# Latent projection with four Strassen pairs, and the queries' norm finished one stage later

## What is computed

```python
u = rms_norm(x, p['norm_g']) * (1.0 + scale[:, None]) + shift[:, None]
proj = u @ p['w_in']
q_a, kv_a, k_rope, z_mla, cb, cc, cx, z_conv, rw, z_rw, g_merge = split_cols(proj)
c_q = rms_norm(q_a, p['q_norm_g'])        # 384 columns
...
ckv = rms_norm(kv_a, p['kv_norm_g'])      # 256 columns
kpe = rope(k_rope[:, :, None, :], pos)[:, :, 0]
...
y_mla = (o_mla * jax.nn.silu(z_mla)) @ p['w_mla_out']     # z_mla: 512 columns
```

## Time and profile before

| | |
|---|---|
| median of 3 runs | 3518.74 us (3515.11 to 3522.74) |
| span of the profiled execution | 3519.6 us |
| busy: PE, PEld, DVE, ACT | 3371.0, 2236.2, 1701.1, 960.9 us |
| mean granted clock of TensorE | 0.972 of full speed |

### The profile page before, as it was taken

The page is one execution under the profiler, slowest core; times in us unless marked ns, Lnnn a source line. Parts: engine busy times, 40 slices in busy tenths (PEclk is TensorE's granted clock), DMA queues, the critical chain, the costliest instruction groups (busy, mean ns, idle before and its releaser), DMA issues. The chain is left out here.

```text
span 3519.6 us, 65817 instructions
## 1 busy us (share of the span) xinstructions
PE 3371.0 (96%) x28655; PEld 2236.2 (64%) x28655; DVE 1701.1 (48%) x3191; ACT 960.9 (27%) x2056; POOL 147.7 (4%) x175
## 2 busy tenths in 40 slices
PE   7999999999989999999989999999999999999998
PEld 5677655666556677765656766566665666776665
DVE  4343044555445788744333420544554467885522
ACT  3201023333245422211122011233332563222201
POOL 1000000000000022100000000000000001220000
PEclk8999999999999999999999999999999998999998
DMA  7112111211220277576011111121112204774521
GB/s 237 37 53 51 36 54 51 58 53 52 52 80 16 109 271 271 187 274 237 11 69 39 51 51 49 42 59 53 52 51 68 57 10 181 277 273 158 183 85 57
DMA packets 250917, 357.00 MB, mean 101 GB/s; under 512 B 47396, under 2 KB 222302, under 8 KB 242055
## 3 DMA queue, kind: packets, MB, share of 16 engines
q1 hardware_dynamic: 217590, 180.49, 17.0%
q0 software_dynamic: 16400, 155.53, 12.0%
q10 hardware_dynamic: 16640, 16.78, 1.5%
HBM read 302.17 MB, written 48.35 MB: 100 GB/s over the span
## 5 line engine op out<-in xcount | busy, mean ns | idle before, releaser
L1226 PE MATMUL rwkv_gate_bank<-u,stream_ring 128*128 128x364 f32 (+1 forms) x2304 | 792.4, 485 | 2.0 <-PEq L1137 2.0
L1226 PEld LDWEIGHTS rwkv_gate_bank<-u,stream_ring 128*128 128x128 f32 x2304 | 415.2, 191 | 220.9 <-issue 11.9
L595 PE MATMUL rwp_b<-u,stream_ring 128*128 128x364 f32 (+1 forms) x864 | 268.3, 473 | 7.2 <-PEq L963 7.2
L2603 PE MATMUL dec_s_bank<-u,att_q_rows 32*64 32x256 f32 x8192 | 244.0, 385 | 0.0
L595 PEld LDWEIGHTS rwp_b<-u,stream_ring 128*128 128x128 f32 x864 | 165.2, 192 | 107.1 <-issue 10.9
L595 PE MATMUL mla_b<-u,stream_ring 128*128 128x364 f32 (+1 forms) x672 | 209.1, 474 | 15.2 <-PEq L2964 8.2
L2990 PE MATMUL out_b<-merged,w_out 128*128 128x364 f32 (+1 forms) x672 | 214.5, 471 | 3.6 <-PEq L2866 3.6
L2603 PEld LDWEIGHTS dec_s_bank<-u,att_q_rows 32*64 32x64 f32 x8192 | 189.0, 134 | 36.6 <-issue 12.3
L595 PEld LDWEIGHTS mla_b<-u,stream_ring 128*128 128x128 f32 x672 | 129.2, 193 | 94.0 <-issue 18.5
L2990 PEld LDWEIGHTS out_b<-merged,w_out 128*128 128x128 f32 x672 | 128.4, 191 | 81.7 <-issue 5.8
L2659 ACT ACTIVATE page_probs<-dec_s_bank,dec_minus_top 128x1024 f32<-128x1024 f32 x64 | 71.3, 1114 | 336.8 <-DVE dec_minus_top L2696 336.8
(11 more groups left out here) (603 smaller groups left out, 5103.4 us busy)
## 6 DMA issues: line engine op xcount, KB each, us to landing
stream_ring<-in_w_in_dram SPq DMA_DIRECT2D x100, 512.0 KB, 4.0
merge_sig<-gates_feature_major SPq DMA_DIRECT2D x16, 1632.0 KB, 9.1
gates_feature_major<-rwkv_gate_stage SPq DMA_DIRECT2D x96, 182.0 KB, 1.9
u<-in_w_ada_dram ACTq DMA_DIRECT2D x16, 1024.0 KB, 12.7
gates_feature_major<-rwkv_gate_stage SPq DMA_DIRECT2D x48, 180.0 KB, 2.0
w_out<-in_w_out_dram SPq DMA_DIRECT2D x14, 512.0 KB, 9.9
start_ada<-in_w_ada_dram SPq DMA_DIRECT2D x6, 1024.0 KB, 11.7
x_feature_major<-o_mla SPq DMA_DIRECT2D x2, 2176.0 KB, 10.3
```

What stands on the lines that cost most here:

```text
L595: mm = pe.matmul(self.banks[j % len(self.banks)][:, 0:m], self.stream.w(c, k), s.u[:, k, t0:t0 + m], start=(k == 0), stop=(k == KD - 1))
L1226: mm = pe.matmul(self.banks[j % 2][:, 0:m], self.stream.w(self.first + n, k), self.s.u[:, k, t0:t0 + m], start=(k == 0), stop=(k == KD - 1))
L2603: mm = pe.matmul(S[64 * half:64 * half + NQ, 512 * i:512 * i + NK], q, keys, start=(cb == 0), stop=(cb == BLOCKS))
```

## The change

The chunks of the mla stage come in another order: the third chunk of q_a and the rope chunk are plain, and then kv_a, the first two of q_a, and the four of z_mla are four pairs, eight passes. The second chunk of the first pair (list index 3) has a buffer of its own (`apart`) in the stage, and is loaded at the stage's begin; the other chunks use the ring. The sums over the squares of ckv are taken behind pass 2, those of the queries behind pass 5. ckv is scaled between passes 5 and 6; the roots of the queries go into a buffer `q_root` that lives over both stages, and the queries are inverted and scaled in the conv stage, by quarters, behind its passes 2, 3, 4 and 5.

```diff
 class WeightStream:
-    NW = 2
+    NW, LONE = 2, 3
...
-        return self.w_in(l, COL_QA, 3) + self.w_in(l, COL_KV, 2) + [rope] + self.w_in(l, COL_ZM, 4)
+        return self.w_in(l, COL_QA + 2 * P, 1) + [rope] + self.w_in(l, COL_KV, 2) + self.w_in(l, COL_QA, 2) + self.w_in(l, COL_ZM, 4)
...
+    def load_apart(self, sp, c, home):
+        self.apart[c] = home
+        sp.dma_start(home, self.chunks[c][0][2]).then_inc(self.apart_landed, 16)
...
-def project_mla(nc, s, l, u_sums):
+def project_mla(nc, s, l, u_sums, q_root):
...
-        pair = PairProjection(ph, s, u_sums, "mla", l, (8,), nbanks, s.o_side[:].rearrange("p k t -> p (k t)"))
+        pair = PairProjection(ph, s, u_sums, "mla", l, (2, 4, 6, 8), [ph.bank(f"p{i}") for i in range(3)], s.o_side[:].rearrange("p k t -> p (k t)"))
...
             def _(sp):
-                for n in range(N_CHUNKS - 2):
-                    pr.load_behind(sp, n)
-                pair.load_behind(sp, 0)
+                s.stream.load_apart(sp, pair.first + 3, apart[:])
+                pr.load_behind(sp, QA2)
+                sp.wait_ge(pr.multiplied, NG * N_SINGLE)
+                s.stream.load(sp, pair.first + 5)
+                sp.wait_ge(pair.made, 7 + 2)
+                sp.wait_ge(pair.summed, 5)
+                s.stream.load(sp, pair.first + 4)
+                for p in range(1, 4):
+                    pair.load_behind(sp, p)
...
             def _(pe):
...
+                pr.multiply(pe, s, QA2)
+                pr.multiply_halves(pe, s, ROPE_CHUNK)
+                pe.wait_ge(sums_made, 2)
+                for i in range(N_PASSES):
                     pair.products(pe, i)
+                    if i == 2:
+                        token_sums(0, sq[:, 3])
+                    if i == 5:
+                        token_sums(1, sq[:, 0])
...
             def _(act):
...
+                act.wait_ge(s.x_stored, 48 * (l + 1))
+                pair.keep_both(act, 0)
+                pair.keep_both(act, 1)
+                for k in range(2):
+                    square(16, 3 + k, s.ckv[:, k])
+                pair.keep_both(act, 2)
+                pair.keep_both(act, 3)
+                roots(0, rstd, KV_LORA)
+                for k in range(2):
+                    square(32, k, s.cq[:, k])
+                for i in range(4, 7):
                     pair.keep_both(act, i)
+                roots(1, q_root, Q_LORA)
+                gates(4)
+                gates(5)
+                pair.keep_both(act, 7)
+                gates(6)
+                gates(7)
...
             def _(dve):
...
+                pair.even_pass(dve, 0, out)
+                pair.odd_pass(dve, 1, out)
+                add_squares(3, 4, NG + 2, 0)
+                pair.even_pass(dve, 2, out)
+                pair.odd_pass(dve, 3, out)
+                dve.wait_ge(rooted, NG)
+                for q in range(4):
+                    part = slice(QUARTER_T * q, QUARTER_T * (q + 1))
+                    dve.reciprocal(rstd[:, part], rstd[:, part]).then_inc(inverted, 1)
+                    if q == 1:
+                        pair.add_both(dve, 4)
+                pair.add_common(dve, 4)
+                add_squares(0, 1, NG + 4, 1)
+                pair.late_half(dve, 4, out(4, 0, pair.late(4)))
+                pair.early_half(dve, 4, out(4, 1, pair.early(4)))
+                add_squares(0, 2, NG + 4, 2)
+                pair.close_first(dve, 4, out(4, 0, pair.early(4)))
+                pair.close_second(dve, 4, out(4, 1, pair.late(4)))
+                pair.odd_pass(dve, 5, out)
+                dve.wait_ge(inverted, 4)
+                for k in range(2):
+                    dve.scalar_tensor_tensor(out=s.ckv[:, k, :], in0=s.ckv[:, k, :], scalar=vec(s, "kv_norm_g", k), in1=rstd[:], op0=ALU.mult, op1=ALU.mult)
+                pair.even_pass(dve, 6, out)
+                pair.even_pass(dve, 7, out)
...
-def project_conv(nc, s, l, u_sums):
+def project_conv(nc, s, l, u_sums, q_root):
...
+                def scale_queries(j):
+                    part = slice(QUARTER_T * j, QUARTER_T * (j + 1))
+                    dve.reciprocal(q_root[:, part], q_root[:, part]).then_inc(q_inverted, 1)
+                    dve.wait_ge(q_inverted, j + 1)
+                    for k in range(Q_LORA // P):
+                        dve.scalar_tensor_tensor(out=s.cq[:, k, part], in0=s.cq[:, k, part], scalar=vec(s, "q_norm_g", k), in1=q_root[:, part],
+                                                 op0=ALU.mult, op1=ALU.mult)
...
-                even_pass(2)
+                pr.even_pass(dve, 2, out)
+                scale_queries(0)
...
-                odd_pass(3)
-                even_pass(4)
-                odd_pass(5)
+                pr.odd_pass(dve, 3, out)
+                scale_queries(1)
+                pr.even_pass(dve, 4, out)
+                scale_queries(2)
+                pr.odd_pass(dve, 5, out)
+                scale_queries(3)
```

More of the change, by code:

```diff
@@ L706, in sum_weights @@
         c = self.first + self.firsts[p]
-        w = lambda chunk, high: self.stream.ring[:, chunk % self.stream.NW, KH_U * high:KH_U * (high + 1), :]
+        w = lambda chunk, high: self.stream.weights(chunk)[:, KH_U * high:KH_U * (high + 1), :]
         a11, a12, a21, a22 = w(c, 0), w(c, 1), w(c + 1, 0), w(c + 1, 1)
@@ L766, in close_second, with even_pass, odd_pass @@
         op.then_inc(self.added, 1)
+    def even_pass(self, dve, i, out):
+        self.add_both(dve, i)
+        self.add_common(dve, i)
+        self.late_half(dve, i, out(i, 0, self.late(i)))
+        self.early_half(dve, i, out(i, 1, self.early(i)))
+        self.close_first(dve, i, out(i, 0, self.early(i)))
+        self.close_second(dve, i, out(i, 1, self.late(i)))
+    def odd_pass(self, dve, i, out):
+        p = i // 2 + 1
+        self.add_both(dve, i)
+        self.add_common(dve, i)
+        self.late_half(dve, i, out(i, 0, self.late(i)))
+        self.early_half(dve, i, out(i, 1, self.early(i)))
+        for j in range(3):
+            self.sum_weights(dve, p, j)
+        self.close_first(dve, i, out(i, 0, self.early(i)))
+        self.sum_weights(dve, p, 3)
+        self.close_second(dve, i, out(i, 1, self.late(i)))
+        self.sum_weights(dve, p, 4)
     def load_behind(self, sp, p):
@@ L842, in _, with square @@
-                for i in range(2):
-                    pair.keep_both(act, i)
-                    for done, k, t0 in ((4, 2, pair.late(i)), (6, 3, pair.early(i)), (7, 2, pair.early(i)), (8, 3, pair.late(i))):
-                        act.wait_ge(pair.added, 8 * i + done)
-                        act.activation(gate(k, t0), gate(k, t0), ACT.Silu)
+                def square(after, to, src):
+                    act.wait_ge(pair.added, after)
+                    act.activation(sq[:, to, :], src, ACT.Square).then_inc(squared, 1)
@@ L858, in _ @@
+                for j in range(5):
+                    pair.sum_weights(dve, 0, j)
+                dve.wait_ge(pr.emptied, NG * N_SINGLE)
                 cos, sin = s.tab["rotary"][64:96, :], s.tab["rotary"][96:128, :]
@@ L870, in _ @@
-                dve.wait_ge(s.x_stored, 48 * (l + 1))
-                for j in range(5):
-                    pair.sum_weights(dve, 0, j)
-                for i in range(2):
-                    pair.add_both(dve, i)
-                    pair.add_common(dve, i)
-                    pair.late_half(dve, i, [(gate(2, pair.late(i)), lambda a: a)])
-                    pair.early_half(dve, i, [(gate(3, pair.early(i)), lambda a: a)])
-                    pair.close_first(dve, i, [(gate(2, pair.early(i)), lambda a: a)])
-                    pair.close_second(dve, i, [(gate(3, pair.late(i)), lambda a: a)])
+                pair.even_pass(dve, 0, out)
```

154 lines of the change are left out of this document (64 added, 90 removed).

## The result

| | before | changed |
|---|---|---|
| median, runs of the same sitting | 3516.93 us (3514.99 to 3522.74, 4 runs) | 3480.09 us (3476.93 to 3485.75, 4 runs) |
| ratio to before | | 0.9892, interval 0.9880 to 0.9904 |
| profiled execution, span | 3519.6 us | 3475.1 us |
| mean granted clock | 0.972 | 0.977 |

The change makes the kernel 1.08% faster: 38 us by the ratio, 37 by the medians. I had forecast 32.1. The direction and the mechanism in the changed stage came out; the size was too small by about 6 us. The ratio's interval is 34 to 42 us. The two profiled executions lie 44.5 us apart, more than the medians, which is the first hint of where the rest is: in something that differs from execution to execution.

What follows compares the result with a forecast made beforehand. TensorE, busy 96% of the span, was taken as the bound. Its gain of 32.8 us, less 0.2 for VectorE and 0.5 for SP, gave -32.1 us and a forecast of 3487 us; own range 3481 to 3492, outer 3479 to 3499.

Steps and rivals of the forecast that it cites:

- Chunks and passes: TensorE in mla, per layer: six plain chunks of 14.62 us go, six passes of 12.83 us come, 10.7 us less.
- The gap: TensorE's idle time in mla ahead of the only pair, 4.06 and 4.07 us, goes, and the slow first product with it.
- The sums of weights: VectorE work after the pair's chunk lands in mla, 3.4 us in all, claimed hidden: 7.5 against 11.2 us.
- VectorE: Norms inside mla and conv passes: TensorE waits 0.1 us per layer in mla's pass 4, between 0 and 0.3; conv nothing.
- SP: Rope's DMAs ahead of the stores of x in the start stage: 0.5 us once, 9.1 at worst.
- rival A: SP ends late in the start stage, held by the rope loads: 3 to 9 us once, 3490 to 3496; chance 10%.
- B: VectorE's inserted norms partly delay TensorE in mla's pass 4 or behind conv's pass 5: 3489 to 3498 us; chance 12%.
- C: Passes in mla run at 1.2 GHz after short stands at bank changes, up to 12.83 us more each; chance 3%.
- D: Mla's head is late by as much as is saved, so TensorE's work does not shorten: 3512 to 3526 us; chance 3%.
- the clock's term: In mla, the pair's slow first product at 1.2 GHz disappears with the idle time: 1.61 and 1.53 us.

## Why the prediction was wrong in size

- **Chunks and passes** (10.7 us per layer) held: eight passes of 12.83 us, no idle time, mla 16.5 and 16.4 us shorter with the gap's part.
- **The gap** went, and the first product is 2.10 us. The sums of weights ended at 82.1 us, before product 3 needed them at 85.00.
- **VectorE** at 0.1 us per layer: nothing was lost. The margin in pass 4 is 0.25 us by the experiment with three more reciprocals, where I had counted a lack of up to 0.3 before overlap. In conv, behind pass 5, `add_common` started at 279.44 and product 6 at 280.63; I had 0.5 us to spare; from its end it was 0.8.
- **SP** at 0.5 us, with 9.1 as the far end: it was held for 12.59 us and cost nothing, since it ended at 55.25, ahead of the 57.1 at which the other engines were done. The pieces did hold SP, as rival A says, but what they hold is not added: the store behind them no longer waits (0.51 in place of 4.37), so SP ends 1.1 us later (55.25 against 54.17) and has 1.9 left.
- **Rivals.** B was excluded by the rows of pass 4, C by the clock of 1.00 over the eight passes, D by the first products, which have no idle time ahead of them. The Trainium skill, TensorE: Matmul & The Clock Gate, section "A second HAM failure mode: psum-queue depth-cycling", would have brought C; the trace disagrees for mla as it did for conv: three banks in turn, and a granted clock of 1.00 from 81 to 189 us.
- **The step that failed** is the clock's term. It read "So the gap goes (4.06 and 4.07), and with it the slow product", and counted 1.61 and 1.53 us. All other clock that TensorE loses was left as it was, at a difference of nothing and without a reason. The runs showed that the same code behind the changed stage loses more or less clock when the work ahead of it moves: conv's first product 0 or 1.7 us, rwp's first chunk 0, 1.7 or 2.7 us, gates and recurrence 511.8 to 519.1 us. In layer 1, in both executions of each program, the changed kernel was on the better side of all three: 1.7 + 1.7 + 2.5 = 5.9 us. Another 0.7 us of the miss are the prices for VectorE and SP that were not paid.
- **How firmly this stands.** That the rows of layer 1 repeat within 0.1 us, and the ratio too (0.9892, 0.9893), shows that part of this deal belongs to the two programs; layer 0 adds a part that differs from execution to execution, 4 us above the forecast in the first profiled pair, 3.6 below it in the second. The measured gains of one and the same change were 38, 35 and 27.5 us, unfilled, with twelve and with six matmuls, around some 33. So the 32.1 fit the change itself, within intervals as wide as 7 us, and the 6 us above them are the luck of where this kernel and the kernel before happened to lie. Which way it would fall could not be read from the profile of before.
- **The range.** 3480.09 lies 0.9 us under the forecast's own range of 3481 to 3492. The outer range of 3479 to 3499 holds it by 1.1 us, which is luck: nothing in it but the spread of executions reached down, and all its rivals cost time. The rows to widen it by were there: a product of 3.79 us at conv's head and a chunk of 16.56 at rwp's, in both layers, 2 x (1.7 + 1.7) = 6.8 us that a shift could give back. With them the low end would have been near 3472.

**What stays open:** what decides whether the clock falls at a given place. The same 3.60 us were followed by no loss, by 1.7 and by 2.7 us; a gap of 4.0 by 1.6 and by 3.15; 1.23 us by 0 and by 1.7; and in the stage of gates and recurrence it fell with no idle time in the rows. Why six matmuls ahead of rwp kept the clock up in that later stage of the kernel before, twelve did not, and six in the changed kernel brought layer 1 to 518.9 us is seen in the rows, not explained. Nor were the borders at mla or attention filled.

## What to carry to other kernels

Take the arithmetic and the waits of a change from the profile, and then look at every border where TensorE stands for a microsecond or more, up and down the program: products that run at half speed there are money that any shift may give or take, and belong in the range, on its low side too. Look at the granted clock inside the long stages as well. When two versions are compared within half a per cent, one comparison is one deal: compare again with some idle matmuls added to both, in more than one number. Here that gave 38, 35 and 27.5 us for the same change, whose sum was 32. Work that is not needed at once (here a norm of queries) is best finished where VectorE has slack: at the stage's end here it made TensorE wait 5.8 us more, and cost 2.8 us of clock on top.

## What the hardware showed that I had not expected

- Idle time of TensorE as short as 1.23 us, with 1.6 us of small transposes behind it, can be followed by work at 1.2 GHz (conv's 3.79 us product), and 3.60 us by work at 2.4 GHz throughout (rwp's 14.87). The loss behind an idle time of 4 to 7 us was 1.6 to 3.2 us.
- The clock also fell with no idle time in the rows, at 64 matmuls of 8 columns, 34 us into gates and recurrence, in six of the eight executions read, and stayed at half for up to 14 us.
- Matmuls without any use, 2.9 us of them in 3.6 us of idle time, once per layer, made a kernel of 3519 us faster by 9 us; twice as many made it no faster (3522).
- SP was held for 12.59 us by four issues into a busy queue, and the store behind them for 0.51; with two issues it was 6.60 and 4.37. The hold looks like a sum over what is queued, not a price for each issue; no run varied it.
